# Token scale of three normalisations taken at the exit from PSUM, with the rows split tile by tile in the stage in front

## The reference

```python
def rmsnorm(x, g):
    y = x * rsqrt(mean(x * x, axis=-1) + EPS)          # one factor per token
    return y * g                                        # one factor per channel

def conv_ffn(xn, buf, w_up, conv_w, conv_b, w_down):
    u = xn @ w_up
    g, v = u[..., :D_FF], u[..., D_FF:]
    gc, new_buf = causal_dwconv(g, buf, conv_w, conv_b) # width 3, along tokens
    return (gelu(gc) * v) @ w_down, new_buf

# layer 0
x = x + rglru_block(rmsnorm(x, a_norm), ...)            # ends in @ a_w_out
x = x + conv_ffn(rmsnorm(x, f_norm[0]), ...)
kv = rmsnorm(x, kv_norm) @ w_kv + b_kv                  # k and v, shared
k = rmsnorm(k, k_norm)
# layer 1
q = rmsnorm(rmsnorm(x, b_norm) @ w_q + b_q, q_norm)
x = x + (attention(q, k, v) @ w_o + b_o)
x = x + conv_ffn(rmsnorm(x, f_norm[1]), ...)
```

## Time and profile before

| | us |
|---|---|
| median of three executions | 2624.71 (2623.25 to 2625.06) |
| the profiled execution | 2623.81 |
| its span in the trace | 2622.0 |
| PE busy | 2494.7 (95%) |
| DVE busy | 1199.3 (46%) |
| ACT busy | 855.9 (33%) |
| POOL busy | 285.5 (11%) |

### The profile page before, as it was taken

How to read it: one execution, slowest core, us unless ns; L and a number is a source line. 1 busy time by engine, 2 the same in 40 slices (tenths; PEclk the granted TensorE clock), 3 DMA queues, 4 the chain that set the end, 5 groups by cost and what they waited for, 6 DMA issues and landing times.

```text
span 2622.0 us, 39675 instructions
## 1 busy us (share of the span) xinstructions
PE 2494.7 (95%) x15088; PEld 2417.9 (92%) x15088; DVE 1199.3 (46%) x1882; ACT 855.9 (33%) x1495; POOL 285.5 (11%) x388
## 2 busy tenths in 40 slices
PE   5999889999999999999999889989999999999998
PEld 4899888999999999999988855989999999999998
DVE  7566555533343333333386776264323333433432
ACT  3455432431331232122244476133213313311211
POOL 2011323000000000000321054230000000000000
PEclk7999989999999999999999998999999999999999
DMA  3111111111111111111152310101111111111112
...
## 3 DMA queue, kind: packets, MB, share of 16 engines
...
q0 software_dynamic: 64, 0.05, 0.0%
...
## 4 chain that ended last, share of the span: by engine, by line
PE 82%; DVE 8%; issue 3%; ACT 3%; DMA 2%; POOL 1%; SPq 0%; ACTq 0%; DVEq 0%; POOLq 0%
PE ps L692 26%; PE ps L694 26%; PE ps L693 26%; PE ps L968 1%; DMA raw<-in_w_q 1%; PE ps L1020 1%; DVE nlo L1518 1%; DVE rstd L1487 1%; DVE convin L1510 1%; DVE y L1510 1%; DVE wlo L1482 1%; PE ps L865 1%; ACT whi L1090 0%; ACT nhi L1111 0%; DVE nlo L1918 0%
## 5 line engine op out<-in xcount | busy, mean ns | idle before, releaser
L692 PE MATMUL ps<-nhi,whi 128*128 128x384 f32 (+1 forms) x3312 | 1098.6, 332 | 63.5 <-POOL nlo L1951 25.0
L694 PE MATMUL ps<-nhi,wlo 128*128 128x384 f32 (+1 forms) x3312 | 1088.9, 329 | 0.0
L693 PE MATMUL ps<-nlo,whi 128*128 128x384 f32 (+1 forms) x3312 | 1088.2, 329 | 0.0
L692 PEld LDWEIGHTS ps<-nhi,whi 128*128 128x128 f32 x3312 | 628.1, 190 | 83.5 <-issue 67.9
L693 PEld LDWEIGHTS ps<-nlo,whi 128*128 128x128 f32 x3312 | 628.7, 190 | 1.6 <-issue 0.2
L694 PEld LDWEIGHTS ps<-nhi,wlo 128*128 128x128 f32 x3312 | 628.2, 190 | 0.0
L1482 DVE TENSOR_TENSOR wlo<-raw,whi 128x1024 fp32r<-128x1024 f32 (+2 forms) x220 | 244.8, 1113 | 622.6 <-ACT whi L1090 622.6
L694 PE MATMUL ps<-hhi,wlo 128*128 128x384 f32 (+1 forms) x1152 | 376.0, 326 | 0.0
L692 PE MATMUL ps<-hhi,whi 128*128 128x384 f32 (+1 forms) x1152 | 375.8, 326 | 0.0
L693 PE MATMUL ps<-hlo,whi 128*128 128x384 f32 (+1 forms) x1152 | 375.7, 326 | 0.0
L1090 ACT ACTIVATE whi<-raw 128x1024 fp32r<-128x1024 f32 (+2 forms) x220 | 208.3, 947 | 447.9 <-PE ps L694 440.2
...
## 6 DMA issues: line engine op xcount, KB each, us to landing
...
```

Source lines behind the costliest of these rows:

```text
L692: pe.matmul(out, whi[s][:, w], mhi[:, k, chunk(c)], start=(k == 0), stop=False)
L693: pe.matmul(out, whi[s][:, w], mlo[:, k, chunk(c)], start=False, stop=False)
L694: last = pe.matmul(out, wlo[s][:, w], mhi[:, k, chunk(c)], start=False, stop=(k == nk - 1))
```

## The change

It concerns the norms ahead of FFN 0, K/V and FFN 1 (not the one ahead of Q).

- x * gain, without rstd, is split in the stage in front. In `residual` ScalarE copies tile kt with the gain as scale into the high part, and VectorE forms x * gain - high as the low part (semaphores xs_hi, xs_lo). This takes k tiles 0 to 5. Tiles 6 and 7 come in the last pair of units, `last_residual`, chunk by chunk.
- rstd is multiplied in behind the matmuls. In an FFN tile VectorE takes the gate half out of PSUM as bank * rstd (`rescaled`, in the place of ScalarE's evac_conv), and multiplies the GELU's result with rstd before it meets the value half. For K and V VectorE takes the banks out with rstd, and ScalarE adds the bias in a pass of its own (`biased`).
- On TensorE the first pair of an FFN is two plain units. The statistics of chunks 1 and 2 are taken inside them, at k = 2 of pieces 0 and 1. K's pair keeps its order chunk by chunk, with the same two places.
- The regions of SBUF are exchanged. Before, nhi and nlo had one region and hhi and hlo another. Now there are two regions of 12 tiles, sa and sb, and one of 4 tiles, sc4, that holds k tiles 6 and 7 of whichever split is in use. FFN 0 reads sb and writes its hidden tiles to sa, FFN 1 the other way round. z, the staging rows, the query, key and bias buffers move accordingly.

The diff, cut to its core:

```diff
-        reg_n = top[0]
-        nhi = take("nhi", [P, KD, T], F32R)
-        nlo = take("nlo", [P, KD, T], F32R)
-        reg_h = top[0]
-        hhi = take("hhi", [P, FB, T], F32R)
-        hlo = take("hlo", [P, FB, T], F32R)
+        reg_a = top[0]
+        sa = take("sa", [P, 2 * FB, T], F32R)
+        reg_c = top[0]
+        sc4 = take("sc4", [P, 4, T], F32R)
+        reg_b = top[0]
+        sb = take("sb", [P, 2 * FB, T], F32R)
+        reg_end = top[0]
...
+            def split_done(p, v=None):
+
+                def before(c, k):
+                    if (c, k) == (0, 0):
+                        pe.wait_ge(xs_lo, xs_tiles(p) + FB)
+                    if k == FB:
+                        pe.wait_ge(xs_lo, xs_tiles(p) + FB + 2 * (c + 1))
+                    if v is not None and k == 2 and c < 2:
+                        stats(v, c + 1)
+                return before
...
                     if first:
-                        first_pair(nb, u, v)
+                        unit(nb, 0, KD, m, split_done(p, v))
+                        unit(nb, 1, KD, m)
...
-            first_pair(N_KV, 2, 2, kv_slots)
+            first_pair(N_KV, split_b, None, 2, kv_slots, split_done(1, 2))
...
-            def residual(n, i, v, last_cols, phase, last=False, u=None):
...
+            def residual(n, i, v, gain, big, last_cols, phase):
 
                 for s in range(2):
                     for c in range(3):
-                        if last and s == 1 and c == 1:
-                            root(v, 0)
-                        if last and s == 1 and c == 2:
-                            norm_hi(u, v, [0], lambda k: prep(n + 1, 1, last_cols, phase) if k == 5 else None)
-                        act.wait_ge(bank_free[3 * s + c], n + 1)
-                        act.wait_ge(sq_added, sq_base(v) + 6 * i + 3 * s + c - 2)
-                        apart()
-                        act.activation(t1[:, chunk(c)].rearrange("p (o t) -> p o t", o=1),
-                                       x[:, ds(2 * i + s, 1), chunk(c)], ACT.Square).then_inc(sq_done, 1)
-                    if not (last and s == 1):
-                        prep(n + 1, s, last_cols, phase)
+                        squared(n, i, v, s, c)
+                    kt = 2 * i + s
+                    act.activation(big[:, ds(kt, 1), :], x[:, ds(kt, 1), :], ACT.Copy, scale=pcol[:, ds(kt, 1), gain])\
+                       .then_inc(xs_hi, 1)
+                    prep(n + 1, s, last_cols, phase)
+            def last_residual(n, v, gain, m, last_cols, phase):
+                i = KD // 2 - 1
+                def highs(c):
+                    for k in range(KD - 2, KD):
+                        act.activation(m[0][k][:, chunk(c)], x[:, k, chunk(c)], ACT.Copy, scale=pcol[:, k, gain:gain + 1])\
+                           .then_inc(xs_hi, 1)
+                for c in range(3):
+                    squared(n, i, v, 0, c)
+                prep(n + 1, 0, last_cols, phase)
+                squared(n, i, v, 1, 0)
+                highs(0)
+                root(v, 0)
+                squared(n, i, v, 1, 1)
+                highs(1)
+                prep(n + 1, 1, last_cols, phase)
+                squared(n, i, v, 1, 2)
+                root(v, 1)
+                highs(2)
+                root(v, 2)
...
-                        evac_conv(0, n, 2, 2 * (KD + f), KD + f)
...
+            def biased(m, s):
+                act.wait_ge(bank_free[3 * s + 2], N_KV + m + 1)
                 bias_s = pcol[:, 2 * m + s, C_BKV:C_BKV + 1]
                 if m == 0:
+                    act.activation(kf[:, s, KS:KT], kf[:, s, KS:KT], ACT.Identity, bias=bias_s).then_inc(kv_biased, 1)
+                    keys = blocks(kf[:, s, 0:KS])[:, :, 1:KB]
+                    act.activation(keys, keys, ACT.Identity, bias=bias_s).then_inc(kv_biased, 1)
                 else:
+                    v = (t1, t2)[s]
+                    act.activation(v[:, :], v[:, :], ACT.Identity, bias=bias_s).then_inc(kv_biased, 1)
...
+                    if low:
+                        p, gain, big = low
+                        kt = 2 * i + s
+                        dve.wait_ge(bank_free[3 * s + 2], n + 1)
+                        dve.wait_ge(xs_hi, xs_tiles(p) + kt + 1)
+                        flat = [t[:, ds(k, 1), :].rearrange("p o t -> p (o t)") for t, k in ((big, FB + kt), (x, kt), (big, kt))]
+                        dve.scalar_tensor_tensor(flat[0], flat[1], pcol[:, ds(kt, 1), gain], flat[2].bitcast(F32),
+                                                 ALU.mult, ALU.subtract).then_inc(xs_lo, 1)
+            def last_residual(n, v, p, gain, m, next_cols, bias_col=None):
+                i = KD // 2 - 1
+                def lows(c):
+                    for k in range(KD - 2, KD):
+                        dve.wait_ge(xs_hi, xs_tiles(p) + FB + 2 * c + k - (KD - 2) + 1)
+                        dve.wait_ge(bank_free[3 + c], n + 1)
+                        dve.scalar_tensor_tensor(m[1][k][:, chunk(c)], x[:, k, chunk(c)], pcol[:, k, gain:gain + 1],
+                                                 m[0][k][:, chunk(c)].bitcast(F32), ALU.mult, ALU.subtract)\
+                           .then_inc(xs_lo, 1)
+                for c in range(3):
+                    added(n, i, 0, c, bias_col)
+                prep(n + 1, 0, next_cols)
+                added(n, i, 1, 0, bias_col)
+                lows(0)
+                recip(v, 0)
+                added(n, i, 1, 1, bias_col)
+                lows(1)
+                added(n, i, 1, 2, bias_col)
+                prep(n + 1, 1, next_cols)
+                recip(v, 1)
+                lows(2)
+                recip(v, 2)
+                seq.settle()
...
+            def rescaled(n):
+                gp, gs = sp_view(convin, FFN_W - 1)
+                for c in range(3):
+                    dve.wait_ge(bank_ready[c], n + 1)
+                    lo, w = CHUNKS[c]
+                    if c == 2:
+                        w = SEQ - lo
+                        dve.tensor_tensor(gs[:, :, FFN_W - 1:], requests(ps[:, c, w:w + NS]), requests(rstd[:, SEQ:T]),
+                                          ALU.mult)
+                    dve.tensor_tensor(gp[:, FFN_W - 1 + lo:FFN_W - 1 + lo + w], ps[:, c, 0:w], rstd[:, lo:lo + w], ALU.mult)\
+                       .then_inc(bank_free[c], 1)
...
+                        dve.wait_ge(conv_done, 2 * (KD + g))
+                        dve.wait_ge(stash_done, KD + g)
+                        rescaled(n)
...
                         dve.wait_ge(gelu_done, g + 1)
+                        seq.mark(dve.tensor_tensor(y[:, :], y[:, :], rstd[:, :], ALU.mult))
+                        seq.settle()
...
+            def kv_out(m, s, c):
+                b = 3 * s + c
+                dve.wait_ge(bank_ready[b], N_KV + m + 1)
+                if m == 1:
+                    dve.tensor_tensor((t1, t2)[s][:, chunk(c)], bank(b, c), rstd[:, chunk(c)], ALU.mult)\
+                       .then_inc(bank_free[b], 1)
+                    return
+                nb = 3 if c < 2 else 2
+                if c == 2:
+                    dve.tensor_tensor(kf[:, s, KS:KT], ps[:, b, 2 * WIN:2 * WIN + NS], rstd[:, SEQ:T], ALU.mult)
+                lo = CHUNKS[c][0]
+                dve.tensor_tensor(blocks(kf[:, s, 0:KS])[:, 3 * c:3 * c + nb, 1:KB],
+                                  ps[:, b, 0:nb * WIN].rearrange("p (b q) -> p b q", b=nb),
+                                  rstd[:, lo:lo + nb * WIN].rearrange("p (b q) -> p b q", b=nb), ALU.mult)\
+                   .then_inc(bank_free[b], 1)
+            for c in range(3):
+                for s in range(2):
+                    kv_out(0, s, c)
...
-                norm(3, C_BN, None, [c], lambda k: prep(N_Q, 0, KD * P) if (c, k) == (0, 6) else None)
+                    kv_out(1, s, c)
+                norm(1, C_BN, None, [c], split_b, lambda k: prep(N_Q, 0, KD * P) if (c, k) == (0, 6) else None)
                 if c == 0:
```

302 lines of the change are left out of this document (143 added, 159 removed).

## The result

| | before | after |
|---|---|---|
| median | 2623.98 us (4 executions, 2622.85 to 2625.06) | 2589.98 us (4 executions, 2589.22 to 2591.95) |
| profiled execution | 2623.81 | 2591.95 |
| its span | 2622.0 | 2589.9 |

A forecast was written before the change was run, and what follows sets the result against it. TensorE, busy 95%, bounds the FFN loops, VectorE the starts behind a norm. Terms -12.6 - 14.0 - 6.9 + 1.1 + 0 = -32.4 us gave a forecast of 2592.3 us, 8-in-10 range 2584 to 2602.

The forecast's parts named there:

- terms 1 and 2: Starts of FFN 0 and FFN 1: first pair at loop time plus two statistic products, -12.6 and -14.0 us.
- steps (a) and (b): FFN 0 start: tiles 0 to 5 split in earlier units; last two split chunk by chunk before k=6.
- rival D: Stage starts: the change does nothing there because another wait already ends with the norm; 2624 us, chance 1%.
- term 3: K/V start: -10.7 us at the pair, +1.85 and +2.0 given back behind it, -6.9 in all.
- Step (1): Behind K's pair: K's separate bias pass delays the strip's DMA and Q's second-side weights behind it, +1.85 us.
- Step (2): Q's norm: V's rescaling enters VectorE's chain, uncovered for chunks 1 and 2, taken as 2.0 us.
- Step (3): Behind Q's norm: V's bias, two passes of 1.1 us, fits in ScalarE's wait for state DMAs, 0.
- Term 4: Out-projection, first unit: ScalarE's scaled copy ahead of the next weight split delays TensorE, +1.1 us, bounds 0 and 3.5.
- Term 5: FFN tiles: VectorE's added work, some 3.1 us per tile, costs TensorE nothing, 0, bounds -0.5 and +3.
- Rival C: FFN block ends: VectorE's chain becomes the bound, slower than before; 2629 us at 10 us added per tile; chance 2%.
- Rival A: Q's start: Q's weights get ahead of the strip, and the saving grows by 4.9 us, 2587.4; chance 20%.
- Rival B: Stage starts: each keeps 3 to 5 us, late steps being TensorE waits that can lower the clock; about 2604; 17%.

The follow-up runs named there:

- e8: Changed kernel with tiles no longer split in the stage in front, rstd still multiplied in at the exit from PSUM: 2603.49 us, ratio 0.9922.
- e3: Changed kernel with V's rescalings of chunks 1 and 2 moved on VectorE to ahead of the second weight split: 2590.97 us, ratio 0.9874.
- e4: Changed kernel with FFN 0's six state DMAs issued between chunks 1 and 2 of Q's norm instead of behind it: 2586.17 us, ratio 0.9857.
- e9: Changed kernel with the product y x rstd of every FFN tile done five times instead of once: 2604.44 us, ratio 0.9926.
- e10: Changed kernel with the product y x rstd of every FFN tile done nine times instead of once: 2681.27 us, ratio 1.0221.
- e1: Changed kernel with the strip's DMA issued by SyncE behind the DMAs of Q's two first weight tiles, instead of by ScalarE: 2586.52 us, ratio 0.9856.
- e7: Changed kernel with VectorE's first reciprocal done three times in a row at all three norms: 2611.15 us, ratio 0.9951.

## Why the prediction was right

*FFN starts, terms 1 and 2.* Forecast -12.6 and -14.0, measured -12.75 and -14.10. The plain pair takes 24.91 and 24.94 us (25.02 forecast), the clock does not fall, and the sum is there 0.20 and 0.17 us ahead of its use, where the text had it on time. e8 shows which part of the change brings it: without the early split the scale at the exit still saves 9.0 and 9.6 us of them. That the rest needs the early split was implied by steps (a) and (b), and e8 is the first run to show it. One reading behind these terms was wrong. The prediction put the late weight split at 471 to 472.6 (rival D) down to VectorE being in the norm. VectorE and ScalarE, timeline before:

```profile
471.14 1.23 DVE L1482 TENSOR_TENSOR wlo<-raw,whi 128x1024 fp32r<-128x1024 f32 x1 [5.29 <-ACT whi L1090]
...
470.03 1.08 ACT L1090 ACTIVATE whi<-raw 128x1024 fp32r<-128x1024 f32 x1
```

VectorE had ended the norm and idled 5.29 us; it waited for ScalarE's copy of the weights, which stood behind the evacuation of the gate banks. In the changed kernel the first unit ends half a pair earlier, and no wait is left at the second pair (462.30). The time came out as forecast, by another way than the one given.

*K/V, term 3, first part.* -10.7 forecast, -10.3 measured. The wait for the sum was 0.77, not 1.3. Not in the forecast were the 0.3 us that TensorE waits for the square of K's heads.

*K/V, what is given back.* +3.85 forecast, +1.95 measured, in two steps. Step (1), the strip, failed: the strip was issued 1.2 us later and ended 1.6 us later against K's head statistic, but the weights of the second side only 0.4. Before, their first packet waited 15 us behind their issue (1345.03 to 1360), and they ended 1.8 us behind the strip; after, they took turns with it nearly from the start and ended 0.5 us behind it. The shift was not passed on one to one. Step (2), V's rescaling, was mis-sized: 2.0 forecast; the way from the copy of the second weight tile to Q's statistic grew by 1.6 (27.44 to 29.01), and e3 gets 1.1 to 1.3 back. Step (3), V's bias at nothing, holds: it runs inside ScalarE's wait for the state DMAs, of which 2.45 us are left behind it, and from their first issue to Q's first evacuation it is 4.7 us before and after (1397.52 to 1402.22, 1378.81 to 1383.50). In e4, which removes that wait, V's bias would be the next to cost time.

*Term 4.* +1.1 forecast, +1.09 in six traces, and 1.4 to 2.4 in the three where the clock fell behind the wait, inside the bound of 3.5.

*Term 5.* 0 forecast; the loop is unchanged, and e9 and e10 measure the cover. Rival C's mechanism is real. Its threshold was about right: the cover is the idle 2.76 us and a lead of 2.1, together 4.9 in the kernel before (3.9 are left in the changed one), where the text had about 5. Its price was too low: with 10.6 us added to the changed kernel the loss is 91 us, 53 of them waits, and the text had 37 at 10, since it priced neither the clock nor the longer tiles.

*Rival A* (2587.4) did not happen, and e1 shows it as 3.6 us, not 4.9. The reasoning for setting it aside was faulty. The earlier trace rows show 12 us in which the weights' queue moved nothing, and the text took this for an engine that does not take turns. In the same trace the two queues moved 264 and 266 packets in 1364 to 1368, and after they do so nearly from the start (122 packets to 312 in 1326 to 1330, 265 to 266 from 1338 on). The Trainium skill, DMA: Bandwidth & Descriptors, section Queues, rings and completion order, says turns packet by packet, and the trace agrees, counted in the profile's packets. Why no packet of the weights moved in the 15 us before 1360 stays open. What the prediction got wrong is what follows from it: a turn is worth a packet whatever it holds, and small packets lose, 0.07 MB against 0.41 in 4 us.

*Rival B*: e7 shows that its premise (each late step is a TensorE wait, and it brings the clock down) holds; the steps were just not late.

*The sum.* Forecast -32.35, measured -32.10 in the profiles: this closeness is partly luck. By the table the rows are off by +1.3 (drift and clock ahead of FFN 0), -0.15, +0.4, -1.9 (what Q's start gives back), +0.7 (no term; the profiles differ by more there without an edit) and -0.1, and these cancel.
